# Memory attention turned round and laced into its neighbours, and latent attention's query rounding moved ahead of weight conversion

## The reference, cut to what matters

```python
h = x @ w_in[l]
c_q, c_kv, k_pe, dq, dk, dv, mq, gate_pre = jnp.split(h, splits, axis=-1)
o_mla = _mla_branch(...)      # "latent" attention, 8 heads, queries and keys of 96, values of 64
o_diff = _diff_branch(...)    # "diff" attention, 8 heads of two softmaxes each
o_mem = _mem_branch(mq, mem, mem_w_kv[l])
g = jax.nn.sigmoid(gate_pre.reshape(b, s, N_BRANCH, d) + b_gate[l])
merged = (g[:, :, 0] * (o_mla @ wb[:MLA_OUT]) + g[:, :, 1] * (o_diff @ wb[MLA_OUT:MLA_OUT + DIFF_OUT])
          + g[:, :, 2] * (o_mem @ wb[MLA_OUT + DIFF_OUT:]))
x = _layernorm(DEEPNORM_ALPHA * x + merged @ w_out[l], ln1_g[l], ln1_b[l])
```

```python
kv = (mem @ w_kv).reshape(b, mem.shape[1], 2, MEM_HEADS, MEM_HD)
sc = jnp.einsum('bqhd,bmhd->bhqm', q, k).astype(jnp.float32) * (MEM_HD ** -0.5)
p = jax.nn.softmax(sc, axis=-1).astype(v.dtype)
return jnp.einsum('bhqm,bmhd->bqhd', p, v).reshape(b, s, MEM_OUT)
```

## Time and profile before

| what | value |
|---|---|
| median of 3 runs | 4833.8 us (4831.41 to 4836.34) |
| the profiled execution | 4837.21 us, its span 4835.4 us |
| granted TensorE clock, mean | 0.898 of full speed |
| TensorE matmuls busy | 87% of the span |
| DVE, ACT, POOL busy | 45%, 30%, 34% |
| second block's first layer: last diff head | 2748.22 to 2780.09 us |
| branch 1 | 2780.09 to 2870.04 us |
| memory heads | 2870.04 to 2992.45 us |
| branch 2 up to the first `w_out` matmul | 2992.45 to 3061.56 us |

### The profile page before, as it was taken

The page is one execution under the profiler, slowest core; times in us unless marked ns, Lnnn a source line. Parts: engine busy times, 40 slices in busy tenths (PEclk is TensorE's granted clock), DMA queues, the critical chain, the costliest instruction groups (busy, mean ns, idle before and its releaser), DMA issues.

```text
span 4835.4 us, 63859 instructions
## 1 busy us (share of the span) xinstructions
PE 4215.7 (87%) x20806; PEld 3480.0 (72%) x20806; DVE 2194.1 (45%) x3452; ACT 1462.0 (30%) x2303; POOL 1638.2 (34%) x2044
## 2 busy tenths in 40 slices
PE   4788878999988879999799898899977998898997
PEld 3577668999976756887576577688755766776885
DVE  5544554333346665235626613433455375235325
ACT  2111112111125543223435522222244354222223
POOL 0011012333321105565142243456521432433654
PEclk6788778999989889999899898899978998888998
DMA  3133201111110002222021121222210211211222
GB/s 127 53 123 131 101 35 53 61 64 62 58 47 18 22 7 83 96 95 83 27 70 49 40 83 57 70 87 95 91 45 27 79 49 40 83 66 61 97 96 86
DMA packets 92779, 328.57 MB, mean 68 GB/s; under 512 B 10240, under 2 KB 12544, under 8 KB 92544
## 3 DMA queue, kind: packets, MB, share of 16 engines
q1 hardware_dynamic: 90928, 323.61, 19.2%
q10 hardware_dynamic: 1616, 1.90, 0.1%
HBM read 323.38 MB, written 2.10 MB: 67 GB/s over the span
## 4 chain that ended last, share of the span: by engine, by line
issue 69%; POOL 30%; POOLq 1%
POOL Wl L259 30%; POOLq L254 0%; POOLq L256 0%; POOLq L259 0%; POOLq L142 0%; POOLq L253 0%; POOLq L2931 0%
## 5 line engine op out<-in xcount | busy, mean ns | idle before, releaser
L259 POOL TENSOR_TENSOR Wl<-raw,Wh 128x256 fp32r<-128x256 f32 x2040 | 1638.0, 834 | 3196.7 <-ACT Wh L351 3196.3
L351 ACT ACTIVATE Wh<-raw 128x1024 fp32r<-128x1024 f32 x510 | 540.2, 1059 | 2083.5 <-PE psum L969 1840.8
L967 PE MATMUL psum<-Hh,Wh 128*128 128x512 f32 (+1 forms) x2704 | 1055.9, 391 | 89.9 <-DVEq L1714 58.7
L968 PE MATMUL psum<-Hl,Wh 128*128 128x512 f32 (+1 forms) x2704 | 1026.9, 380 | 0.0
L969 PE MATMUL psum<-Hh,Wl 128*128 128x512 f32 (+1 forms) x2704 | 1025.7, 379 | 0.0
L967 PE MATMUL psum<-Gh,Wh 128*128 128x512 f32 (+3 forms) x1968 | 736.7, 374 | 33.1 <-DVEq L1714 29.6
L969 PE MATMUL psum<-Gh,Wl 128*128 128x512 f32 (+3 forms) x1968 | 729.2, 371 | 0.0
L968 PE MATMUL psum<-Gl,Wh 128*128 128x512 f32 (+3 forms) x1968 | 728.9, 370 | 0.0
L967 PEld LDWEIGHTS psum<-Hh,Wh 128*128 128x128 f32 x2704 | 524.7, 194 | 227.9 <-issue 78.7
L969 PEld LDWEIGHTS psum<-Hh,Wl 128*128 128x128 f32 x2704 | 524.8, 194 | 74.2
L968 PEld LDWEIGHTS psum<-Hl,Wh 128*128 128x128 f32 x2704 | 526.5, 195 | 70.1 <-issue 4.0
(11 more groups left out here) (326 smaller groups left out, 5249.0 us busy)
## 6 DMA issues: line engine op xcount, KB each, us to landing
raw<-in_wstream SPq DMA_DIRECT2D x510, 512.0 KB, 3.2
stage<-in_ada SPq DMA_DIRECT2D x80, 512.0 KB, 4.1
M<-in_ada SPq DMA_DIRECT2D x16, 512.0 KB, 5.6
X<-in_xT SPq DMA_DIRECT2D x1, 2048.0 KB, 12.6
out<-X SPq DMA_DIRECT2D x8, 256.0 KB, 2.0
X<-in_ctxT SPq DMA_DIRECT2D x1, 1024.0 KB, 7.7
M<-in_memT ACTq DMA_DIRECT2D x1, 1024.0 KB, 6.5
M<-in_axial ACTq DMA_DIRECT2D x1, 512.0 KB, 3.5
```

The lines of the kernel that those rows point to most:

```text
L259: last = pool.tensor_tensor(Wl[:, s, c], raw[:, s, c], Wh[:, s, c].bitcast(F32), ALU.subtract)
L351: act.activation(Wh[:, s], raw[:, s], ACT.Copy).then_inc(v["w_high"], 1)
L967: pe.matmul(dst, a[0], b[0], start=first, stop=False)
L968: pe.matmul(dst, a[0], b[1], start=False, stop=False)
```

## The change

There are three parts, all in the second block, so each happens twice in a run (once a layer).

1. **Memory attention** gets the form of the other two. The scores are computed once, with queries on partitions (12 matmuls of 256 columns), DVE takes maxima, ACT exponentials with their sums, DVE divides the weights, TensorE transposes them, and the output product follows (6 matmuls of 512 columns). Values are projected like keys (24 matmuls of 256 columns) and transposed. The diagonal, the second scores, the sums by matmul and the large reciprocal are gone. The loop is written out.
2. **Projections across the borders.** The first memory head's key, value and query projections and branch 1's first gate tile stand in the last diff head, where other heads have their next head's projections; branch 1's second gate tile stands right behind it. Branch 1's first two output tiles are computed up to the last head's part (k = 7), then the wait for that head, then the rest. The query, key and value projections of memory heads 1 to 3 stand between the steps of the head before, branch 2's first two gate tiles in the last memory head, and branch 2's first output tiles are finished in the same split way. Branch 1 now takes its tiles in the order gate, gate, output, output in place of gate, output. The weight stream is laid out to match. The diff heads' diagonal has a buffer of its own and no longer lies in `hand`, where the gates' sigmoids go.
3. **Latent attention.** ACT rounds the next head's queries ahead of the four tiles of weights and DVE subtracts them there too; ACT's `next_weights` moves from the middle of the head to its end.

The core of the diff:

```diff
@@ latent_act
         act.activation(X[:, r:r + 2, 0:CTX], psum[:, b, :]..., ACT.Copy).then_inc(v["raw_done"], 1)
-        next_weights()
...
         high_values()
-        high_weights(0)
-        high_weights(1)
         if more:
             high_queries()
-        high_weights(2)
-        high_weights(3)
+        for qt in range(4):
+            high_weights(qt)
+        if more:
+            next_weights()
@@ latent_dve
         low_values()
-        low_weights(0)
-        low_weights(1)
         if more:
             low_queries()
-        low_weights(2)
-        low_weights(3)
+        for qt in range(4):
+            low_weights(qt)
@@ diff_pe
         if more:
             next_projection()
+        else:
+            from_memory()
+            from_memory()
...
-        if more:
-            next_projection()
+        next_projection()
...
-        if more:
-            values_around(4 * h + 3)
-        else:
-            turned_weights(4 * h + 3)
+        values_around(4 * h + 3)
...
+    turned_memory()
+    next_projection()
     square_sums()
-    spread_roots()
+    return last_spread
@@ memory_pe (new)
+    for h in range(4):
+        more = h < 3
+        scores(h)
+        from_queries()
+        turned_weights(h)
+        if more:
+            from_memory()
+            from_memory()
+        else:
+            from_queries()
+        output(h)
+        if more:
+            turned_values()
@@ branch on TensorE
+        if begun:
+            ks = range(4) if paired else range(KT)
+            w = weights(2 * P) if paired else None
+            ws = [...] if paired else [weights(), weights()]
+            beside = between()
+            banks = []
+            for j in range(2):
+                banks.append(tiles.take(pe))
+                for k in ks[:-1]:
+                    mm3(psum[:, banks[j], :], ..., k == 0, False)
+                if j == 0 and beside:
+                    beside()
+            wait_ready()
+            for j in range(2):
+                mm3(psum[:, banks[j], :], ..., False, True).then_inc(tile_done, 1)
@@ memory_act (new)
+    for h in range(4):
+        more = h < 3
+        exps(h)
+        if more:
+            high_queries()
+        else:
+            gate(2, 0)
+        high_weights(h, 0)
+        high_weights(h, 1)
+        if more:
+            high_keys()
+            raw_values()
+        else:
+            gate(2, 1)
+        high_output(h)
+        if more:
+            high_values()
```

More of the change, by code:

```diff
@@ L458, in mlp @@
                     updated_squares(m, segs)
[L460 to L479, removed]
         def last_weights():
@@ L613, in second_act @@
     latent_act(act, v, tiles, from_bank, next_weights, diff_counts)
-    branch(0, True)
-    diff_act(act, v, tiles, next_weights, diff_counts)
-    branch(1, False)
[L618 to L623, removed]
-    branch(2, True)
+    branch(0, True, False)
+    diff_act(act, v, tiles, next_weights, gate_from, diff_counts)
+    branch(1, False, True)
+    memory_act(act, v, tiles, next_weights, gate, diff_counts)
+    branch(2, True, True)
     for m in range(KT):
@@ L1599, in values_around, with from_memory, turned_memory, last_spread @@
         mm.then_inc(v["tile_done"], 1)
+    def from_memory():
+        project(weights(), slice(0, P), (v["Gh"], v["Gl"]), 0, CTX)
+    def turned_memory():
+        b = tiles.take(pe)
+        pe.wait_ge(v["raw_done"], counts.raw_done.next(3))
+        for tt in range(2):
+            mm = pe.transpose(psum[:, b, tt * P:(tt + 1) * P], X[:, 6, tt * P:(tt + 1) * P], ident)
+        mm.then_inc(v["tile_done"], 1)
+    def last_spread():
+        b = tiles.take(pe)
+        def issue():
+            pe.wait_ge(v["diag_ready"], counts.diag_ready.next())
+            pe.matmul(psum[:, b, :], ones, diag[:].rearrange("p b q -> p (b q)"), start=True, stop=True).then_inc(v["tile_done"], 1)
+        return issue
     next_projection()
@@ L1651, in branch @@
         else:
-            project(weights(), slice(0, P), G, X0, SEQ)
+            for _ in range(2):
+                project(weights(), slice(0, P), G, X0, SEQ)
 def dve_program(nc, block, v, a, out):
@@ L2720, in diff_dve @@
         combine(4 * h + 1)
-        if more:
+        raw_taken(look())
+        if not more:
             raw_taken(look())
@@ L2744, in diff_dve @@
             low_output(h - 1)
+        if not more:
+            for_pe()
         low_weights(3, look())
@@ L2751, in diff_dve @@
             operands_complete()
+        else:
+            low_memory()
+            operands_complete()
+            first = gate()
         b = look()
```

432 lines of the change are left out of this document (266 added, 166 removed).

## The result

| | before | changed |
|---|---|---|
| median of four runs | 4835.07 us (4831.41 to 4839.55) | 4678.2 us (4676.6 to 4679.8) |
| profiled execution | 4837.21 us, span 4835.4 | 4679.8 us, span 4678.0 |
| mean granted clock | 0.898 | 0.916 |

The ratio is 0.9675, with a 95% interval from 0.9658 to 0.9692: 3.2% less time. The forecast was 4660 us in a range of 4620 to 4700, so the direction, the size and the range held, and 18 us of the forecast gain did not come. The rest of this document is about where the 157 us came from and where the 18 stayed.

What follows compares the result with a forecast made beforehand. TensorE was taken to be idle or slow-clocked in the last diff head, memory heads and latent query waits. 4837.2 - 145.6 - 30 = 4661.6 us, 4658 on the median's scale, rounded up to 4660; range 4620 to 4700.

Steps and rivals of the forecast that it cites:

- Last diff head: Last differential head, including the second gate tile and square sums: 37 us a layer, mostly at full clock.
- Branch 1: Stretch after the last differential head, up to the first memory scores: 81.9 us a layer.
- the new wait at the closing matmuls: After the first two output tiles, no weight slot is free earlier, so TensorE waits 3.4 us, plus 2 for lower clock.
- the wait for the last head is hidden: Before the first output tiles close: roots, scaling, splits and sigmoid take 8 us, the 42 matmuls ahead 9.5.
- Memory heads: Four memory attention heads: 16.0 us each for the first three, 14.6 for the last, 62.6 a layer against 122.41.
- The chain behind the scores: In a memory head, maximum, exponentials, reciprocal, divisions and signals take about 4 us, hidden by 5.44 us of query projection.
- The rival of a head bound by its own chain: Memory heads stay as long as before, 30.6 us each and not 15.7: 119 us more, 4780 us; chance 6%.
- Branch 2: Stretch after the memory heads, through the unchanged 3.65 us wait at `w_out`: 58.0 us a layer, no wait after closing matmuls.
- Latent attention: Latent stage: earlier queries shorten steady heads from 19.4 to 16.9 or 17.7 us; 15 us a layer, 30 in all.
- the end of the last head: Last latent head's end, counted together with six steady heads as a saving of 17.5 or 11.6 us a layer.
- The rival of half clock in dense stretches: Filled stretches from last differential heads to `w_out` run at half clock: 450 us more, 5110 us; chance 2%.
- The sum with 3.2 us for every block: POOL needs 3.2 us and not 2.8 per weight block, each conversion wait grows 0.4: 4 us more in all.

Runs made afterwards that it cites:

- the kernel without interleaving: Changed kernel with the memory heads' projections put behind each head instead of between its scores, transposes and output; 4758.1 us.
- the kernel with the second weights late: Changed kernel, but in the memory stage's first output projection TensorE takes the second output weight block only in front of the second output tile; 4661.9 us.
- the latent part undone: Changed kernel with the latent attention edit taken back (order of the next queries and place of the next output weights' conversion), memory stage kept; 4707.7 us.
- the next weights put back: Changed kernel with only the conversion of the next head's output weights moved back behind ACT's raw value copy; 4681.5 us.

## Why the prediction was right, and where it was not

**Last diff head: right.** Forecast 37 us, measured 37.05 and 37.09, at a clock of 1.00. The wait for POOL ahead of the memory queries was there, 1.17 us where 1.7 was forecast; one of 1.26 us for POOL ahead of branch 1's first gate tile (where other heads have their value tile) was not foreseen, and the output still started at 27.7 us (28 forecast).

**Branch 1: the term that failed.** Forecast 81.9 us, measured 89.45 and 89.31. The prediction had counted the new wait at the closing matmuls (3.4 us, measured 3.98) and allowed 2 us for the clock behind it (measured 3.0). Its step that the wait for the last head is hidden was right, but it went from there to a first output tile that starts at once, and did not follow the two weight blocks that TensorE takes ahead of it. The second of them had its slot from the second gate tile, so its low part could not be ready: 3.73 us, and 1.4 us of low clock. That this is the cause, and not the roots or the first block, is shown by taking the second block late: the wait vanished. The slot rule that the prediction used correctly for the closing matmuls (no slot is free until its block is done with) would have shown this wait too. Of the 18 us by which the forecast was off, this stretch is 15.

**Memory heads: right in mechanism and size.** Forecast 62.6, measured 63.3 and 63.7; heads 16.2 us apart (16.0 forecast), the wait for POOL 0.86, 0.78 and 0.86 us (0.8), neither transposes nor output waiting for the chain. The chain behind the scores was taken as 4 us; the kernel without interleaving shows it openly, 4.0 us in the head above and 3.6 to 4.6 over the four. The rival of a head bound by its own chain (30.6 us a head) is out even there: heads without any cover are 26.2 to 27.0 us apart.

**Branch 2: right.** 58.0 forecast, 58.2 measured, with no wait behind its closing matmuls and the 3.65 us at `w_out` unchanged.

**Latent attention: right in mechanism, the size 1 to 2 us a layer too large.** Forecast 15 a layer, measured 13.0 and 13.1, and 14.1 on the mean of the 14 stretches. The wait went, the low part moved by what was said, the maximum follows VectorE's last subtraction. The prediction gave 16.9 us a head at full clock and 17.7 at half clock. Of the first layer's eight heads four have their scores at full clock (3.02 us for the group) and four at half clock (5.48), and from the second head's scores to the last's a head takes 17.4 on the mean. Where all seven heads behind the first run at full clock, as in the kernel with the second weights late, it is 17.1. In the heads at full clock the time goes to the wait for ACT's raw queries, 1.4 to 1.5 us, which the prediction named as the thing that keeps the rest of the head as long as it was. So the six steady heads gave 12.3 us (116.6 less 104.3), between its 10.2 and 15. The term that failed is the end of the last head: it was counted as 1.4 to 2.5 us less, and from the last head's scores to branch 0 it is 21.1 us where it was 20.5, 0.6 more. The first head, for which there was no term, gave 1.3 and covers half of what this end fell short. The statement that the moved `next_weights` costs nothing was true but short: the move gains 2 to 3 us a layer.

**The rest** was 3.1 us shorter, mostly diff heads 0 to 6 (230.8 to 228.2 us in the first layer, 229.3 to 228.2 in the second), which no term had. No run shows why, and stretches of the same code differ by as much between executions.

**The sum again.** Branch 1 2 x 7.5, memory heads and branch 2 2 x 1.1, latent 2 x 2.0, less 3.1 for the rest: 18.1, and the forecast was missed by 18.2. That the two agree is no test, since the rest is what remained of the total; but every error except this rest went the same way, so the range held without large errors cancelling. Two readings of the working were slightly off and move nothing: the row that it gives as 2.79 us for POOL says 2.82, and its terms for the last diff head's output add up to 28.9 and not 28.8.

**The rival of half clock in dense stretches** is out: the clock rose to 1.00 in all stretches that were filled. This is also where the rule on activity that the prediction took from the Trainium skill, "TensorE: Matmul & The Clock Gate" (What's actually happening), was tested, and the trace agrees.

**POOL's pace.** The sum with 3.2 us for every block, which the prediction left in its range, did not come: the three value blocks of the memory heads took 2.82 us each, with VectorE idle beside them. Behind it stood the rule of the Trainium skill's "GPSIMD Engine Reference" (1. Specifications) that VectorE's steps of two SBUF inputs or in a two-port mode disturb POOL; the trace agrees: the block behind the last diff head took 3.21 us beside the roots' diagonal (0.77 us on VectorE, both operands in SBUF), one beside a subtraction that reads PSUM took 2.82.

## What to carry to other kernels

When a wait is computed for a step that takes several buffers, follow each buffer to the step that frees its slot, and take each just ahead of its own use: a block taken one tile too early cost some 6 us a layer here (6.5 against this one profile), more than its wait of 3.73, because the clock fell behind it. A split finish that hides a chain of 5.7 us of waits by holding two tiles and both weight slots open can cost more than the chain; one open tile, with the roots taken earlier, hid the same chain with no wait left. And when filling a stalled stretch, the largest gain is in laying work of known length over a known chain (41 us of 65 a layer here), which can be counted ahead from one engine's list and the other engines' durations.

## What the runs showed of the hardware

The lower clock behind a wait has no fixed price, even for the same code. Five profiles (the changed kernel twice, the latent part undone, the next weights put back, the memory not interleaved) have the waits of 3.73 and 3.98 us in both layers. Behind the second the 48 matmuls took 13.8 us in seven of the ten places and 12.6 in three; at full clock they take 10.88. So the 12.62 us of the kernel with the second weights late needs no other cause than this. The rows of one of the three, the second layer with the latent part undone, both waits and the start of the tile behind the 48 matmuls:

```profile
4019.52 0.79 PE L1040 MATMUL psum<-Gh,Wh 128*128 128x512 f32 x1 [3.73 <-POOL Wl L259]
...
4038.45 0.49 PE L1040 MATMUL psum<-Hh,Wh 128*128 128x512 f32 x1 [3.99 <-POOL Wl L259]
...
4051.06 0.39 PE L1040 MATMUL psum<-Gh,Wh 128*128 128x512 f32 x1
```

With them the stretch from the last diff head to the memory heads varies from 125.4 to 126.8 us. The waits of 0.8 us in the memory heads left the clock at 1.00 in the window.

The latent stage, where TensorE waits several times a head, varies in the same way: with the same code it took 139.5 to 141.8 us, and its groups of scores stand at half clock in one execution and at full clock in the next. The first latent scores, with the same code ahead of them, began between 2272.0 and 2278.3 us in the seven profiles, at 2277.95 and 2273.77 in the two of the changed kernel; the shift builds up in many small steps and not at one wait. No run here explains it, and differences under 5 us between medians are therefore read here from windows of the stage that was edited, and against this scatter.
